# The first selection of expert rows in one run on VectorE, and the output projection's halves behind the first expert sums

## The reference

```
y   = concat(retention(h, ctx), differential_attention(h, ctx))   # 4 heads each
x   = x + mod2 * (y @ w_out)
h2  = modulate(x, norm2_g, mod3, mod4)
q   = (h2 @ w_query) -> (tokens, 8 heads, 2 halves, 128)
s   = q . sub_keys                      # 128 scores for each half
v1, i1 = top_k(s[half 0], 16);  v2, i2 = top_k(s[half 1], 16)
best, pos = top_k(v1[:, None] + v2[None, :], 16)
experts = i1 * 128 + i2 at pos;  gate = softmax(best)
out = sum_k gate_k * gelu(expert_u[experts_k] . h2) * expert_v[experts_k]
```

## Time and profile before

| | |
|---|---|
| time, median of 3 runs | 1736.1 us (1735.23 to 1738.25) |
| time of the profiled execution | 1736.14 us |
| its span, first to last instruction | 1734.3 us |
| mean granted TensorE clock | 0.937 |
| TensorE busy | 1528.3 us (88% of the span) |
| VectorE busy | 749.8 us (43%) |
| ScalarE busy | 500.7 us (29%) |
| GpSimd busy | 289.9 us (17%) |
| bytes moved | 586.83 MB, mean 338 GB/s |
| the gathers | 256, L1613, 270.75 MB |
| chain that ended last | PE 70%, DMA 18%, DVE 6% |

### The profile page before, as it was taken

The page is one execution under the profiler, slowest core; times in us unless marked ns, Lnnn a source line. Parts: engine busy times, 40 slices in busy tenths (PEclk is TensorE's granted clock), DMA queues, the critical chain, the costliest instruction groups (busy, mean ns, idle before and its releaser), DMA issues.

```text
span 1734.3 us, 15575 instructions
## 1 busy us (share of the span) xinstructions
PE 1528.3 (88%) x5474; PEld 730.9 (42%) x5474; DVE 749.8 (43%) x1807; ACT 500.7 (29%) x1283; POOL 289.9 (17%) x268
## 2 busy tenths in 40 slices
PE   7999997796469896797999797799999999999998
PEld 3444453463134541333443333343344444455443
DVE  3653157866785566556425446532312100031101
ACT  3311224332432233314344134433412110122210
POOL 1000003324443333323112212221000000000000
PEclk9999998898579988897999998899999999999999
DMA  9555437999999999999999999999876677855774
GB/s 352 209 183 194 170 110 279 420 420 421 421 386 422 421 421 421 419 421 422 405 422 420 421 421 421 421 421 421 350 302 261 242 292 279 313 215 225 289 296 187
DMA packets 93869, 586.83 MB, mean 338 GB/s; under 512 B 6960, under 2 KB 6960, under 8 KB 28128
## 3 DMA queue, kind: packets, MB, share of 16 engines
q1 hardware_dynamic: 55632, 311.94, 46.0%
q0 software_dynamic: 37584, 270.75, 37.8%
q10 hardware_dynamic: 576, 3.15, 0.5%
HBM read 584.76 MB, written 1.05 MB: 338 GB/s over the span
## 4 chain that ended last, share of the span: by engine, by line
PE 70%; DMA 18%; DVE 6%; issue 3%; ACT 2%; SPq 1%; POOL 0%; POOLq 0%; DVEq 0%; ACTq 0%
PE bank L982 35%; DMA arena<-in_peer_rows,pidx 10%; PE bank L1060 7%; PE bank L682 7%; DMA ring<-in_weights 6%; PE bank L1140 5%; PE bank L760 2%; PE bank L947 2%; PE bank L989 2%; DVE arena L2084 2%; PE bank L958 2%; PE bank L737 2%; DMA ring<-in_w_mod 1%; DMA spare<-in_peer_rows,pidx 1%; PE bank L1042 1%
## 5 line engine op out<-in xcount | busy, mean ns | idle before, releaser
L1613 POOL DMA_INDIRECT arena<-in_peer_rows,pidx x227 | 252.0, 1110 | 588.8 <-PE bank L1140 535.4
L2084 DVE SCALAR_TENSOR_TENSOR arena<-arena,ring 128x1024 f32<-128x1024 f32 x227 | 273.4, 1223 | 112.7 <-DMA arena<-in_peer_rows,pidx 110.6
L982 PE MATMUL bank<-ring,arena 128*128 128x512 f32 x736 | 319.4, 593 | 0.0
L982 PE MATMUL bank<-ring,hT_all 128*128 128x512 f32 x544 | 246.1, 608 | 14.8 <-issue 10.5
L1140 PE MATMUL bank<-arena,keep 128*32 128x512 f32 x908 | 160.2, 705 | 105.7 <-ACT keep L1571 105.7
L982 PEld LDWEIGHTS bank<-ring,arena 128*128 128x128 f32 x736 | 138.5, 190 | 168.8 <-issue 168.7
L982 PEld LDWEIGHTS bank<-ring,hT_all 128*128 128x128 f32 x544 | 103.6, 195 | 151.0 <-issue 141.9
L1558 ACT ACTIVATE pf<-pf 128x2 f32<-128x2 f32 x128 | 25.9, 202 | 402.8 <-DVE arena L2084 367.7
L2205 DVE TENSOR_TENSOR x_all<-x_all,bank 128x512 f32<-128x512 f32 x40 | 27.5, 687 | 208.3 <-PE bank L1060 113.9
L1140 PEld LDWEIGHTS bank<-arena,keep 128*32 128x32 f32 x908 | 21.5, 115 | 176.1 <-ACT keep L1571 138.9
L682 PE MATMUL bank<-ring,hT_all 128*128 128x512 f32 x192 | 86.9, 609 | 1.5 <-DVE hT_all L1690 1.5
(11 more groups left out here) (377 smaller groups left out, 1696.7 us busy)
## 6 DMA issues: line engine op xcount, KB each, us to landing
ring<-in_weights SPq DMA_DIRECT2D x122, 2048.0 KB
ring<-in_w_mod SPq DMA_DIRECT2D x12, 2048.0 KB
ring<-in_w_in SPq DMA_DIRECT2D x6, 2048.0 KB
ring<-in_weights SPq DMA_DIRECT2D x8, 1024.0 KB
ring<-in_weights SPq DMA_DIRECT2D x8, 512.0 KB
arena<-in_peer_rows,pidx POOLq DMA_INDIRECT x227, 15.4
mem_all<-in_b_mod POOLq DMA_DIRECT2D x3, 512.0 KB, 10.9
hT_all<-in_xT ACTq DMA_DIRECT2D x1, 1024.0 KB, 7.8
```

The costliest lines, as they stand in the source:

```text
L982: m = mm(b[:, :], src[:, k], slot8[w][:, k], start=(k == 0), stop=(k == KC - 1))
L1613: nc.gpsimd.indirect_dma_start(out=row_in[n % SLOTS], out_offset=None, in_=a["peer_rows"], in_offset=bass.IndirectOffsetOnAxis(ap=pidx[:, ...
L2084: stt(uslot[n % SLOTS], uslot[n % SLOTS], 1.0, h2g[n % 4], ALU.mult, ALU.mult, accum_out=pact2[:, 16 * (g % 2) + k:16 * (g % 2) + k + 1]). ...
```

## The change

Three orders are changed and nothing is computed differently. VectorE: `h2_turn(0)` goes ahead of `diff_max(1, 0)`; the first selection, from the key copy through the decays to `select(0)`, stands in one run, and `diff_max(1, 2)`, `diff_mix(1, 1)` and all later softmax steps of tile 1 stand behind it. ScalarE: its copies, exponentials and squares are put in the order that goes with this. TensorE: `keep_warm(2)` goes; `diff_turn(1, 0)` and the keys of head 0 stand ahead of the retention scores; `regroup(0)` stands ahead of `diff_turn(1, 1)`; the turn `md1` no longer stands behind the first half of the output projection, which moves into `PICK_WORK[2]`, between the picks of gathers 0 and 1 and those of 2 and 3. The second half stays at 4. `UNITS` follows these orders.

```diff
--- before.py
+++ after.py
@@ -179,7 +179,7 @@
     return 112 if c == 8 else 16 * (c - 1) + 2
 
 
-PICK_WORK = {4: ["out 1", "regroup 1"], 6: ["query q02"], 8: ["keys 02", "query q03"], 10: ["keys 03"], 16: ["h2_turns 1"],
+PICK_WORK = {2: ["out 0"], 4: ["out 1", "regroup 1"], 6: ["query q02"], 8: ["keys 02", "query q03"], 10: ["keys 03"], 16: ["h2_turns 1"],
              18: ["regroup 2", "query q10"], 20: ["row r10", "row r11", "keys 10", "query q11"], 22: ["keys 11", "query q12"], 24: ["keys 12", "query q13"],
              26: ["keys 13", "query q4"], 28: ["keys 04", "keys 14"], 30: ["query q5"], 32: ["keys 05", "keys 15"],
              36: ["query q6"], 38: ["keys 06", "keys 16"], 42: ["query q7"], 44: ["keys 07", "keys 17"], 58: ["mean nm"]}
@@ -248,6 +248,8 @@
         return [("g" + what, "D")]
     if kind in ("row", "mean"):
         return [(what, "D")]
+    if kind == "out" and what == "0":
+        return [("o1a", "D"), ("o1b", "D")]
     if kind == "repeat":
         return [(f"e{what}a", "A"), (f"e{what}b", "D")]
     if kind == "mkey":
@@ -276,8 +278,8 @@
 for _e, _names in (("D", "nx nc c4x0"), ("A", "c4x1"), ("D", "c4k0"), ("A", "c4k1 c3x0 c3x1 c0x0"), ("D", "c0x1"), ("A", "c0k"), ("D", "r8 r9"),
                    ("A", "s00a s00b c5x0"), ("D", "c5x1"), ("A", "s01a s01b c5k0"), ("D", "c5k1"), ("A", "s02a s02b"), ("D", "r4 r5 p00 p01"),
                    ("A", "s03a s03b"), ("D", "p02 p03"), ("A", "c1x0 c1x1"), ("D", "r6 r7"), ("A", "c1k0"), ("D", "c1k1"), ("A", "c2x0"),
-                   ("D", "o0a o0b"), ("A", "c2x1 s10a s10b s11a s11b"), ("A", "q00"), ("D", "p10 p11 k00 p12 p13"),
-                   ("A", "s12a s12b q01 s13a s13b"), ("D", "k01 g0"), ("A", "e00a e00b e01a e01b e02a e02b e03a e03b"), ("D", "o1a o1b")):
+                   ("D", "o0a o0b"), ("A", "c2x1 s10a s10b s11a s11b"), ("A", "q00"), ("D", "k00 p10 p11 p12 p13"),
+                   ("A", "s12a s12b q01"), ("D", "g0"), ("A", "s13a s13b"), ("D", "k01"), ("A", "e00a e00b e01a e01b e02a e02b e03a e03b")):
     UNITS += [(n, _e) for n in _names.split()]
 for _n in sorted(PICK_WORK):
     for _w in PICK_WORK[_n]:
@@ -900,31 +902,26 @@
             diff_scores(1, 0)
             diff_scores(1, 1)
             h2_turns(0)
-            keep_warm(2)
             query("q00", 0, slice(0, P))
-            ret_scores(1, 0)
-            ret_scores(1, 1)
+            diff_turn(1, 0)
             key_scores(0, 0)
-            diff_turn(1, 0)
+            for h in range(RH):
+                ret_scores(1, h)
             mod_rows(10, cpad)
-            ret_values(1, 0)
-            ret_values(1, 1)
-            ret_scores(1, 2)
-            ret_scores(1, 3)
             diff_scores(1, 2)
-            ret_values(1, 2)
-            ret_values(1, 3)
+            for h in range(RH):
+                ret_values(1, h)
             query("q01", 1, slice(0, P))
-            diff_scores(1, 3)
+            regroup(0)
             diff_turn(1, 1)
             diff_values(1, 0)
+            diff_scores(1, 3)
             mod_rows(11, cpad)
             key_scores(0, 1)
             diff_turn(1, 2)
             diff_values(1, 1)
-            regroup(0)
+            diff_turn(1, 3)
             diff_values(1, 2)
-            diff_turn(1, 3)
             repeat_tokens(0, 0)
             diff_values(1, 3)
             repeat_tokens(0, 1)
@@ -932,9 +929,6 @@
             turn_blocks(turn("mr1"), [PR[:, 1, c * P:(c + 1) * P] for c in range(4)])
             repeat_tokens(0, 2)
             repeat_tokens(0, 3)
-            open_unit("o1a")
-            open_unit("o1b")
-            out_half(1, range(0, 4))
             pe.wait_ge(sem("mix_diff"), 2)
             turn_blocks(turn("md1"), [PR[:, 1, 2048 + c * P:2048 + (c + 1) * P] for c in range(4)])
 
@@ -1106,6 +1100,9 @@
                 if kind == "h2_turns":
                     h2_turns(1)
                 elif kind == "out":
+                    if what == "0":
+                        open_unit("o1a")
+                        open_unit("o1b")
                     out_half(1, range(4 * int(what), 4 * int(what) + 4))
                 elif kind == "query":
                     t = int(what[1]) if len(what) == 3 else None
@@ -1379,23 +1376,23 @@
             h2_square(0)
             h2_root(0)
             unit_copy("c2x1", PR[:, 1, 1024:1536], ACT.Silu)
+            h2_turn(0)
             diff_exps(1, 0)
-            h2_turn(0)
             diff_exps(1, 1)
             query_copy("q00")
             act.dma_start(g5early, a["b_mod"].flatten()[5 * D:6 * D].partition_broadcast(P)).then_inc(sem("g5_in"), 16)
             diff_copy(1, 0)
+            gate_exp(0)
+            out_squares(2, M[0], (ret_out, 8))
+            diff_copy(1, 1)
             diff_exps(1, 2)
-            gate_exp(0)
             query_copy("q01")
             diff_exps(1, 3)
-            diff_copy(1, 1)
-            out_squares(2, M[0], (ret_out, 8))
             diff_copy(1, 2)
             out_root(2)
             repeat_copy(0, 0)
+            out_squares(3, M[1], (diff_out, 8))
             repeat_copy(0, 1)
-            out_squares(3, M[1], (diff_out, 8))
             out_root(3)
             mix_turn("mr", 1)
             repeat_copy(0, 2)
@@ -2040,35 +2037,33 @@
             residual_out(0)
             h2_mean(0)
             h2_apply(0)
+            h2_turn(0)
             diff_max(1, 0)
-            h2_turn(0)
             diff_max(1, 1)
             diff_mix(1, 0)
-            diff_mix(1, 1)
-            decay(1, 0)
-            decay(1, 1)
             key_copy(0, 0)
             half_top(0, 0)
             half_top(0, 1)
-            decay(1, 2)
-            decay(1, 3)
-            diff_max(1, 2)
+            for h in range(RH):
+                decay(1, h)
             best_pairs(0)
             next_pairs(0)
+            pair_rows(0, 0)
+            pair_rows(0, 1)
+            spread(0)
+            select(0)
+            diff_max(1, 2)
+            diff_mix(1, 1)
+            on_mod(10)
             diff_mix(1, 2)
             diff_max(1, 3)
-            on_mod(10)
-            pair_rows(0, 0)
+            on_mod(11)
             out_mean(2)
-            pair_rows(0, 1)
-            spread(0)
             key_copy(0, 1)
-            select(0)
-            on_mod(11)
             diff_mix(1, 3)
             diff_copy(1, 3)
+            half_top(1, 0)
             mix_ret(1, 2)
-            half_top(1, 0)
             half_top(1, 1)
             best_pairs(1)
             out_mean(3)
```

## The result

Eight runs of the changed kernel have a median of 1742.08 us (1740.2 to 1746.35), beside 1736.34 us (1734.27 to 1738.3) for the kernel before on the same chip. The ratio is 1.0034, 95% interval 1.0025 to 1.0044: slower by 5.9 us (4.3 to 7.6).

A forecast was written before the change was run, and what follows sets the result against it. Transfers bound the long stretch to 1240 us, TensorE the rest; the change acts at 237 to 320 us. Gather 0 at 267.3 plus holes of 10.4 gave 277.8 against 273.9, +3.9: 1740.0 us, 8-in-10 range 1732 to 1744.

The forecast's parts named there:

- The place of the first query: TensorE's first query starts at 241.4 us instead of 240.93, after 3.0 us idle where `keep_warm(2)` ran.
- Its clock: TensorE's first query runs at half clock behind the idle hole, costing 1.7 us.
- The selection in one run: On VectorE, the pure selection after the half tops takes 7.6 us against 12.3, 4.7 us off.
- Gather 0: First gather on GpSimd's queue: issued at 267.3 us, 2.5 earlier; at full clock 265.6, 4.2 earlier.
- What is then late: Softmax steps of tile 1 behind the select: `at13` ends at 277.5, gather 4 goes at 277.6, full-clock holes sum to 7.2.
- The tail: First picks after a 4.4 us hole; they and the output half cost another 2.7 at half clock; picks 4 and 5 at 314.0.
- The sum: Gather 0 plus later holes: 277.8 against 273.9, +3.9 us at half clock; +0.6 at full clock.
- Early start carried through: Rival: gathers 3, 4 and 5 released in time, `at13` ends by 275.5, 1731.8 us; chance 0.17.
- Clock stays up: Rival: TensorE's clock does not fall, holes eat the gain, +0.6, 1736.7 us; chance 0.23 together with absorption.
- Absorption by the end: Rival: the slip is real but the end hides it, 1736 to 1738 us; chance 0.23 together with clock up.
- The late `wq 1`: Rival: late `wq 1` also holds `q02`, queries and picks shift by another 3, 1743.5 us; chance 0.10.
- What would show it: Signs: gather 0 at 265 to 268, DMA share under 0.9, clock 0.50 in three places, picks 4 and 5 at 311 to 315.

The follow-up runs named there:

- e11: The kernel before without its two keep-warm matmuls ahead of the first query, nothing else changed: 1736.52 us, ratio 1.0002 to the kernel before.
- e1: The changed kernel with the two keep-warm matmuls put back ahead of the first query: 1741.94 us, ratio 1.0027 to the kernel before.
- e10: e4 with the two keep-warm matmuls back before the first query: 1739.39 us, ratio 1.0016 to the kernel before.
- e12: e5 with the two keep-warm matmuls, first output half still behind picks 0 and 1: 1736.43 us, ratio 1.0000 to the kernel before.
- e9: The changed kernel with keep-warm matmuls: two before the first query, two ahead of the regroup, three behind it: 1739.98 us, ratio 1.0020 to the kernel before.
- e5: The changed kernel with tile 1's softmax steps pulled ahead again, into times when VectorE waits: 1738.29 us, ratio 1.0005 to the kernel before.
- e6: e12 with the turn `md1` ahead of the first output half and that half ahead of the picks: 1734.50 us, ratio 0.9985 to the kernel before.
- e2: The kernel before with only the change's moves of the first output half and `md1`: 1736.66 us, ratio 1.0000 to the kernel before.
- e8: The changed kernel with the old tail, first output half ahead of `md1` and both ahead of the picks: 1746.18 us, ratio 1.0050 to the kernel before.
- e3: The kernel before with one pair swapped, the turn `md1` ahead of the first output half: 1735.41 us, ratio 0.9992 to the kernel before.
- e4: The changed kernel with the first output half ahead of the picks again, but behind `md1`: 1740.54 us, ratio 1.0027 to the kernel before.

## Why the prediction was right, and where its sizes were off

The changed kernel is slower, by 5.9 us where 3.9 were forecast, within the range. The mechanism that was forecast is there at each step, but the sum was split wrongly between the order and the clock.

*The place of the first query.* Forecast at 241.4, 4.06 behind the h2 turns, with 3.0 us idle. Found: 4.13 and 3.04.

*Its clock.* Forecast: 1.7 us at half clock. In the profiled execution it took 2.60. It is not a constant: 2.60, 1.63 and twice nothing, in four profiles with the same hole, and 1.63 behind 2.50 in e11, against 3.81 us, the full clock, in all nine profiles with a hole of 0.8 or 1.3. The Trainium skill ("TensorE: Matmul & The Clock Gate", Part 1, on the HAM clock gate) says of the start of a kernel that the number of matmuls at the low rate differs between runs of one kernel; these rows show the like in the middle of one. In time, the pair is worth 1.2, 1.9, 0.9 and 0.3 us in four pairs of kernels (e1, e10, e12, e11), each alone within its uncertainty, all of one sign.

*The selection in one run.* Forecast 7.6 us from the first step behind the decays to the end of the spread. Found: 260.55 to 268.13, 7.6.

*Gather 0.* Forecast 2.5 us earlier, or 4.2 at full clock. Found 1.5 with the slow query and 3.8 to 4.1 with a fast one.

*What is then late.* Forecast: the softmax steps behind the select make `at13` and gather 4 late, 277.6 at full clock, 279.8 with the query's 1.7 and the further 0.5. Found, with the h2 turns moved to where they are in the profile before: 278.4 in e9, where the clock stayed up, 279.6 in e1, 281.5 in the changed kernel. e5, e12 and e6 show that these steps are the cause, about 5 us of time.

*The tail.* Forecast: 4.4 us of waiting ahead of the first picks, picks 4 and 5 at 314.0. Found: 4.05, and 314.9 (317.08 less 2.22). The half took 9.09 us, 2.0 more than at full clock. The kernel before pays nearly as much, at its second half:

```profile
300.81 8.55 PE L737 MATMUL bank<-ring,s_all 128*128 128x512 f32 x16
```

Its halves take 7.11 + 8.55 = 15.66 us, those of the changed kernel 9.09 + 7.13 = 16.22, 0.56 more. The new tail is worth nothing in the old order (e2); in the new order it may be better than the old one (e8, 2.8 us, within the uncertainty). The half ahead of the picks but behind `md1` was faster each time it was tried, by 1.4 us in e3, 1.2 in e4, 1.9 from e1 to e10 and 2.6 from e12 to e6, each by itself within or at the edge of what a run can tell.

*The sum.* Start plus holes gave +3.9; the data row gives 4.9, the issues 5.6, the times 5.9 (4.3 to 7.6). In the profiled execution 0.9 of the difference is the first query. The forecast split the sum into 3.3 for the clock (1.7 + 0.5 + 2.7 in the new order, less 1.7 that the old order pays too, with rounding) and 0.6 for the order. e9 tests the split: its clock fell only at the first picks and the half, so by these terms it should lie at 0.6 + 2.7 - 1.7 = 1.6. Measured: 3.5 (1.9 to 5.0). In its profile, with the h2 turns moved, gather 0 is where the full clock had it, 265.7 for 265.6, but gathers 4, 5, 7 and 9 come 0.8, 0.9, 1.0 and 1.6 later than the forecast's 277.6, 281.4, 288.4 and 293.8: the holes between the softmax steps were taken too short. Of the 3.5 the clock's part at the tail is about 0.5 (the halves' 9.00 + 7.13 against 15.66), so the order costs about 3 us, an estimate, where 0.6 was forecast. The clock costs about 3 as well: that 0.5 and the 2.4 that both fillings gave back, against the forecast's 3.3. That the total came into the range with the order mis-sized this far is in part luck. No run held the clock up everywhere in the new order, so the order's part was not measured by itself.

Two slips in the working changed little. 7.24 MB are 17.1 us at full rate, which in 20.2 us leaves 3.1 from the issue to full rate, not 2.7. And the holes at full clock sum to 7.1, not 7.2.

*The rivals.* Early start carried through needed `at13` by 275.5: it began at 280.0 (282.26 less 2.22). With the order of e6 gather 4 is issued at 272.8 on the same time scale, and the gain is 2.6 instead of 4.3 us; it is not the early start's alone, as e12, which differs from e6 only in having the first output half behind picks 0 and 1, gained nothing. Clock stays up: it did not, and e9, nearest to it, lies at 3.5 and not 0.6. Absorption by the end: not seen, +5.6 at gather 27, +6.2 at the end of the span and 5.9 in the times. The late `wq 1` held nothing in the changed kernel's profile, where `q02` follows picks 4 and 5 at once; it does in e5 and e12, where those picks come earlier.

*What would show it.* DMA share under 0.9, the three stretches at 0.50, the slow half and picks at 311 to 315 are all there; gather 0 lies 0.3 outside its 265 to 268 (268.3).

## What to carry to other kernels

An earlier start of the engine that bounds a stretch is worth what its next requests can keep up with: before pulling its first request forward, list who releases the second to the eighth, and move only steps that none of these need. Work that waits behind such a run belongs into the waits inside it, as the maximum and the copy between the decays in e6 do. And compare two profiles only from a common point just ahead of the change, here the h2 turns, or an accident upstream of 2.2 us is read as an effect.

## What the runs showed of the hardware

The same idle time of 3.04 us ahead of the same 32 matmuls left TensorE's clock at 1.00 in two profiles and took it to 0.50 for part or all of them in two others, so one profile cannot price it; the standard deviation of the timed runs was 2.0 to 2.7 us in the kernels with this hole or one of 2.50, and 1.3 to 1.8 in those with the pair in its place. A filling that was longer than its hole cost more than the clock it saved: eight keep-warm matmuls took 8.43 us in 4.04, and gather 4 came 3.1 us later. A gather 0 that started 1.6 us later cost nothing measurable where gather 5 waited for something else anyway (e11), while 6.6 us at gather 4 went with 5.9 us of time in the changed kernel; it is no rule, as 4.7 there went with 2.8 in e10. And from gather 27 to the end of the span, through unchanged work, profiled executions gained up to 1.4 or lost up to 4.2 us against the kernel before.
